# An SSD scan that keeps its outputs feature-major: decay matrix as moving side, cumulative decays spread by four products, norm by a product

## What is computed

```python
def step(h, inp):
    xc, dtc, bc, cc = inp
    cum = jnp.cumsum(dtc * a, axis=1)
    xdt = xc * dtc[..., None]
    diff = cum[:, :, None, :] - cum[:, None, :, :]
    lmat = jnp.where(tri, jnp.exp(jnp.where(tri, diff, 0.0)), 0.0)
    cb = jnp.repeat(jnp.einsum('btgn,bsgn->btsg', cc, bc), hg, axis=-1)
    y = jnp.einsum('btsh,bshp->bthp', cb * lmat, xdt) \
        + jnp.einsum('bthn,bhpn->bthp', ch, h) * jnp.exp(cum)[..., None]
    decay_out = jnp.exp(cum[:, -1:, :] - cum)
    h = h * jnp.exp(cum[:, -1])[:, :, None, None] \
        + jnp.einsum('bshn,bshp->bhpn', bh * decay_out[..., None], xdt)
    return h, y
```

## Time and profile before

| what | value |
|---|---|
| median of 3 runs | 1685.81 us (1683.71 to 1687.26) |
| the profiled execution | 1686.15 us |
| its span | 1684.3 us |
| busy in the span | PE 1557.0 (92%), DVE 771.6 (46%), ACT 629.2 (37%), POOL 421.4 (25%) |
| scan block | 836.6 to 1002.2 us of the span |
| busy in the scan block | PE 148.53, DVE 130.03, ACT 84.80, POOL 129.19 of 165.60 us |
| chunk loop | 838.0 to 966 us, then the samples |

### The profile page before, as it was taken

How to read it: one execution, slowest core, us unless ns; L and a number is a source line. 1 busy time by engine, 2 the same in 40 slices (tenths; PEclk the granted TensorE clock), 3 DMA queues, 4 the chain that set the end, 5 groups by cost and what they waited for, 6 DMA issues and landing times. The chain is left out here.

```text
span 1684.3 us, 27825 instructions
## 1 busy us (share of the span) xinstructions
PE 1557.0 (92%) x11737; PEld 1296.0 (77%) x11737; DVE 771.6 (46%) x1255; ACT 629.2 (37%) x1203; POOL 421.4 (25%) x261
## 2 busy tenths in 40 slices
PE   4899988999999899999999959998999999979897
PEld 4588766666666689999987738776999998965666
DVE  3443311465666576650098855233421422048533
ACT  4334211455555452222246543333430421226521
POOL 1142001111000022331189835121121121203422
PEclk9999998999999999999999989998999999999999
DMA  9322336412111011111110156112100135220222
...
DMA packets 125921, 129.95 MB, mean 77 GB/s; under 512 B 16824, under 2 KB 100202, under 8 KB 125670
## 3 DMA queue, kind: packets, MB, share of 16 engines
...
...
## 5 line engine op out<-in xcount | busy, mean ns | idle before, releaser
L154 PE MATMUL banks<-h_T_rest,w_ssd_high 128*128 128x352 f32 x480 | 156.0, 325 | 0.0
L154 PE MATMUL banks<-h_T_high,w_ssd_high 128*128 128x352 f32 x480 | 155.8, 325 | 0.0
L154 PE MATMUL banks<-h_T_high,w_ssd_rest 128*128 128x352 f32 x480 | 155.2, 323 | 0.0
L154 PE MATMUL banks<-out_even_w_high,mix_parts 128*128 128x512 f32 x384 | 121.9, 395 | 8.9 <-DVE out_even_w_rest L2355 8.9
L154 PE MATMUL banks<-h_T_high,w_qk_high 128*128 128x352 f32 x384 | 125.5, 327 | 0.6 <-issue 0.6
L154 PE MATMUL banks<-h_T_high,w_qk_rest 128*128 128x352 f32 x384 | 123.3, 321 | 0.0
L154 PE MATMUL banks<-h_T_rest,w_qk_high 128*128 128x352 f32 x384 | 123.2, 321 | 0.0
L1403 DVE TENSOR_REDUCE pe_T<-banks 128x1 f32<-128x512 f32 (+7 forms) x108 | 81.9, 764 | 37.4 <-PE banks L154 36.8
L1630 POOL TENSOR_TENSOR w_ssd_rest<-w_ssd,w_ssd_high 128x1024 fp32r<-128x1024 f32 x20 | 58.8, 2941 | 137.1 <-ACT w_ssd_high L1583 137.1
L154 PEld LDWEIGHTS banks<-out_even_w_high,mix_parts 128*128 128x128 f32 x384 | 73.0, 190 | 25.6 <-issue 10.4
L1320 ACT ACTIVATE p_att<-banks,pe_T 128x512 f32<-128x512 f32 (+7 forms) x128 | 86.2, 680 | 15.7 <-DVE pe_T L1403 14.8
...
## 6 DMA issues: line engine op xcount, KB each, us to landing
...
```

The source lines that it names most:

```text
L154: return nc.tensor.matmul(out, lhsT, rhs, start=start, stop=stop, skip_group_check=True)
```

## The change

Nothing else than the scan block changes, but for `S.dta`, which has a 10th column of zeros at its end.

- The decay matrix becomes the moving side of intra and x dt the stationary one, two heads of 64 features in each output tile; inter takes h as the stationary side. So y comes out feature-major, `gated_T`. exp(cum) for it is made by ScalarE from the cum banks (`from_start`, four activations of 64x512 a chunk) into `decay_from_start`, and VectorE's first product L2116 takes it as a full tile.
- The cumulative decays are spread otherwise: one product for each group of four heads makes them as rows in the cb bank; VectorE multiplies them with a pattern (`sums`, L2064) into `cum_by_head`; four products with a stationary side of ones, 32 rows each, spread them over the partitions. The mask product is gone; VectorE subtracts with a floor at zero (min with 0), in one instruction for each head, 16 of 128x128 (L2079), each with a per-partition scalar; the triangle is put into C.B by VectorE (L2066).
- z is neither turned nor copied: GpSimd gates `gated_T` with `S.zT` directly. The yT turns are gone too. x D goes into intra as eight products with diagonal matrices (made once, in front of the loop, by GpSimd).
- The norm: ScalarE squares `gated_T` (`squares`), TensorE sums it over the features with a stationary side of ones (`sum`, eight products into a 128x128 bank, which each partition then holds), VectorE scales it and takes the reciprocal, 128x128, ScalarE the root, 128x128, and `put_y` applies it in eight instructions of 128x128 (L2058) with the weight as a per-partition scalar.
- Of the weights products heads 0 to 7 stay on VectorE (L2085), heads 8 to 15 go to GpSimd (L2009).
- SyncE's loads of the samples' states wait for the gating of their chunk in place of z's turn.

```diff
-        order = [(u, 0) for u in AHEAD]
+        order = [(u, 0) for u in FIRST]
         for i in range(NTP):
-            order += [(u, i + 1) for u in AHEAD if i + 1 < NTP] if i + 1 < NTP else [("sp", 0)]
-            order += [(u, i if u != "yT" else i - 2) for u in UNITS if not (u == "yT" and i < 2)]
+            if i + 1 < NTP:
+order += [("cb", i + 1), ("xs", i + 1), ("inter", i), ("cum0", i + 1), ("cum1", i + 1)]
+            else:
+order += [("sp", 0), ("inter", i)]
+            order += [("intra", i), ("upd", i)] + ([("sum", i - 1)] if i else [])
...
+        for q in range(4):
+            mm(nc, e.ps[row(q), b, 288:288 + P], S.dta[:, i:i + 3, :].rearrange("p i h -> p (i h)")[:, 4 * q:4 * q + 32], e.F["tri"], True, True)
...
     elif u in ("cum0", "cum1"):
-        for hh in range(8):
-            hd = 8 * int(u[3]) + hh
-            mm(nc, e.ps[:, b + hh // 4, (hh % 4) * P:(hh % 4 + 1) * P], S.dta[:, i, hd:hd + 1].broadcast_to([P, P]), e.F["tri"], hh % 4 == 0, False)
-            if hh % 4 == 3:
-                last = mm(nc, e.ps[:, b + hh // 4, :].rearrange("p (h t) -> p h t", h=4), e.identb, e.B["later"][:, None, :].broadcast_to([P, 4, P]), False, True)
-    elif u == "z":
-        for j in range(8):
-            last = nc.tensor.transpose(e.ps[:, b + j // 4, (j % 4) * P:(j % 4 + 1) * P], S.zT[:, j, tok], e.ident)
+        pe.wait_ge(heads_ready, i + 1)
+        for q in (0, 1) if u == "cum0" else (2, 3):
+            last = mm(nc, e.ps[:, b + q % 2, :], ones[row(q), :], heads[row(q), :, :], True, True)
     elif u == "inter":
         pe.wait_ge(h_ready, i + 1)
-        for g in range(G):
-            last = mm(nc, e.ps[:, b + g, :], S.convT[:, 10 + g, tok], h[:, g * 512:(g + 1) * 512], True, True)
+        for j in range(8):
+            last = mm(nc, e.ps[:, b + j // 4, j % 4 * P:(j % 4 + 1) * P], h[:, j * P:(j + 1) * P], S.convT[:, 10 + j // 4, tok], True, True)
     elif u == "intra":
         pe.wait_ge(xdt_ready, i + 1)
-        for hd in range(SH):
-            if hd % 8 == 0:
-                pe.wait_ge(W_ready, 2 * i + hd // 8 + 1)
-            last = mm(nc, e.ps[:, b + hd // 8, (hd % 8) * SP_:(hd % 8 + 1) * SP_], L[:, i % 2, hd // 8, hd % 8, :],
-                      xdt[:, i % 2, hd * SP_:(hd + 1) * SP_], True, True)
+        if i == 0:
+            pe.wait_ge(d_ready, 1)
+        pe.wait_ge(W_dve, i + 1)
+        for j in range(8):
+            if j == 4:
+                pe.wait_ge(W_pool, i + 1)
+            out_j = e.ps[:, b + j // 4, j % 4 * P:(j % 4 + 1) * P]
+            mm(nc, out_j, diag_d[:, j, :], S.convT[:, j, tok], j % 4 == 0, False)
+            for x in range(2):
+                hd = 2 * j + x
+                last = mm(nc, out_j[x * SP_:(x + 1) * SP_, :], xdt[:, i % 2, hd * SP_:(hd + 1) * SP_], L[:, i % 2, hd // 8, hd % 8, :], False, j % 4 == 3)
...
-    elif u == "yT":
-        pe.wait_ge(yn_ready, i + 1)
+    elif u == "sum":
+        pe.wait_ge(y_squared, i + 1)
         for j in range(8):
-            last = nc.tensor.transpose(e.ps[:, b + j // 4, (j % 4) * P:(j % 4 + 1) * P], y[:, i % 3, j * P:(j + 1) * P], e.ident)
...
+    nc.scalar.activation(sm[:, i % 2, 1:3, :], sm[:, i % 2, 1:3, :], ACT.Exp).then_inc(decays, 1)
+def from_start(i):
+    if i >= 2:
+        act.wait_ge(taken["inter", "dve"], i - 1)
+    for c in range(2):
+        act.wait_ge(done[f"cum{c}"], i + 1)
+        src = both(f"cum{c}", i).rearrange("p b (j x t) -> p (b j) x t", x=2, t=P)
+        for x in range(2):
+            half = slice(x * SP_, (x + 1) * SP_)
+            last = nc.scalar.activation(E[half, i % 2, c * 512:(c + 1) * 512].rearrange("p (j t) -> p j t", j=4), src[half, :, x, :], ACT.Exp)
+        last.then_inc(taken[f"cum{c}", "act"], 1)
...
-def gate_rows(i):
-    act.wait_ge(done["z"], i + 1)
-    nc.scalar.copy(zs[:, i % 2, :].rearrange("p (b n) -> p b n", b=2), both("z", i)).then_inc(taken["z", "act"], 1)
-def norm(i):
+def squares(i):
     act.wait_ge(y_gated, i + 1)
-    nc.scalar.activation(zs[:, i % 2, :], y[:, i % 3, :], ACT.Square, accum_out=ss[:, i % 2, :]).then_inc(y_squared, 1)
+    if i:
+        act.wait_ge(done["sum"], i)
+    nc.scalar.activation(sq, y[:, i % 3, :, :], ACT.Square).then_inc(y_squared, 1)
+def root(i):
     act.wait_ge(var_ready, i + 1)
     nc.scalar.activation(ss[:, i % 2, :], ss[:, i % 2, :], ACT.Sqrt).then_inc(std_ready, 1)
-    act.wait_ge(std_ready, i + 1)
-    nc.scalar.activation(y[:, i % 3, :], y[:, i % 3, :], ACT.Copy, scale=ss[:, i % 2, :]).then_inc(yn_ready, 1)
...
 copies(0)
+from_start(0)
+decay(0)
 for i in range(NTP):
     if i + 1 < NTP:
         copies(i + 1)
     else:
         sample_copies()
-    gate_rows(i)
     if i:
-        norm(i - 1)
+        squares(i - 1)
+    if i + 1 < NTP:
+        from_start(i + 1)
+        decay(i + 1)
+    if i >= 2:
+        root(i - 2)
 act.wait_ge(done["out"], 1)
-act.wait_ge(y_gated, NTP - 1)
-nc.scalar.copy(zs[:, 0, :].rearrange("p (b n) -> p b n", b=2), both("out", 0)).then_inc(taken["out", "act"], 1)
+nc.scalar.copy(E[:, 0, :].rearrange("p (b n) -> p b n", b=2), both("out", 0)).then_inc(taken["out", "act"], 1)
+squares(NTP - 1)
...
+def weights(i):
+    k = i % 2
+    pool.wait_ge(L_ready, 2 * i + 2)
+    nc.gpsimd.tensor_tensor(L[:, k, 1, :, :], L[:, k, 1, :, :], cc[:, k, P:2 * P][:, None, :].broadcast_to([P, 8, P]), ALU.mult).then_inc(W_pool, 1)
...
-    yi = y[:, i % 3, :]
+    yi = y[:, i % 3, :, :]
     pool.wait_ge(taken["intra", "dve"], i + 1)
-    link(nc.gpsimd.tensor_tensor(yi, yi, xsb[:, i % 3, :], ALU.add))
-    pool.wait_ge(taken["z", "act"], i + 1)
-    nc.gpsimd.tensor_tensor(yi, yi, zs[:, i % 2, :], ALU.mult).then_inc(y_gated, 1)
+    nc.gpsimd.tensor_tensor(yi, yi, S.zT[:, :, i * P:(i + 1) * P], ALU.mult).then_inc(y_gated, 1)
...
-def put_yT(i):
-    dve.wait_ge(done["yT"], i + 1)
-    s = VEC["ssd_norm"][0]
-    nc.vector.tensor_tensor(S.convT[:, 0:8, i * P:(i + 1) * P], both("yT", i).rearrange("p b (j t) -> p (b j) t", j=4),
-                            e.vec[:, s:s + 8][:, :, None].broadcast_to([P, 8, P]), ALU.mult).then_inc(taken["yT", "dve"], 1)
 def variance(i):
-    dve.wait_ge(y_squared, i + 1)
-    link(nc.vector.tensor_scalar(ss[:, i % 2, :], ss[:, i % 2, :], 1.0 / SI, EPS, ALU.mult, ALU.add))
+    dve.wait_ge(done["sum"], i + 1)
+    nc.vector.tensor_scalar(ss[:, i % 2, :], e.ps[:, pair[("sum", i)], 0:P], 1.0 / SI, EPS, ALU.mult, ALU.add).then_inc(taken["sum", "dve"], 1)
+    dve.wait_ge(taken["sum", "dve"], i + 1)
     nc.vector.reciprocal(ss[:, i % 2, :], ss[:, i % 2, :]).then_inc(var_ready, 1)
+def put_y(i):
+    dve.wait_ge(std_ready, i + 1)
+    for j in range(8):
+        nc.vector.scalar_tensor_tensor(S.convT[:, j, i * P:(i + 1) * P], y[:, i % 3, j, :], e.vec[:, norm_w + j:norm_w + j + 1], ss[:, i % 2, :], ALU.mult, ALU.mult)
+def sums(i):
+    k = i % 2
+    dve.wait_ge(done["cb"], i + 1)
+    b = pair[("cb", i)]
+    nc.vector.tensor_tensor(heads[:, :, :], e.ps[:, b, 288:288 + P][:, None, :].broadcast_to([P, 4, P]), e.F["fold"][:, 0:4][:, :, None].broadcast_to([P, 4, P]), ALU.mult).then_inc(heads_ready, 1)
+    nc.vector.tensor_copy(cc[:, k, 256:288], e.ps[:, b, 256:288])
+    nc.vector.tensor_tensor(cc[:, k, 0:256].rearrange("p (g t) -> p g t", g=G), e.ps[:, b, 0:256].rearrange("p (g t) -> p g t", g=G),
+                            e.F["tri"][:, None, :].broadcast_to([P, G, P]), ALU.mult).then_inc(taken["cb", "dve"], 1)
+    dve.wait_ge(taken["cb", "dve"], i + 1)
+    nc.vector.tensor_copy(sm[:, k, 2, :], cc[:, k, 272:288])
+    nc.vector.tensor_tensor(sm[:, k, 1, :], cc[:, k, 272:288], cc[:, k, 256:272], ALU.subtract).then_inc(small, 1)
 def differences(i):
     k = i % 2
-    dve.wait_ge(done["cb"], i + 1)
-    nc.vector.tensor_copy(cc[:, k, :], e.ps[:, pair[("cb", i)], 0:288]).then_inc(taken["cb", "dve"], 1)
-    dve.wait_ge(taken["cb", "dve"], i + 1)
-    nc.vector.tensor_copy(sm[:, k, 0, :], cc[:, k, 256:272])
-    nc.vector.tensor_copy(sm[:, k, 2, :], cc[:, k, 272:288])
-    nc.vector.tensor_tensor(sm[:, k, 1, :], cc[:, k, 272:288], cc[:, k, 256:272], ALU.subtract).then_inc(small, 1)
     for c in range(2):
         dve.wait_ge(done[f"cum{c}"], i + 1)
-        nc.vector.tensor_tensor(L[:, k, c, :, :], both(f"cum{c}", i).rearrange("p b (h t) -> p (b h) t", h=4),
-                                cc[:, k, 256 + 8 * c:264 + 8 * c][:, :, None].broadcast_to([P, 8, P]), ALU.subtract).then_inc(taken[f"cum{c}", "dve"], 1)
-def weights(i, c):
+        dve.wait_ge(taken[f"cum{c}", "act"], i + 1)
+        src = both(f"cum{c}", i).rearrange("p b (h t) -> p (b h) t", h=4)
+        for x in range(8):
+            last = nc.vector.tensor_scalar(L[:, k, c, x, :], src[:, x, :], cc[:, k, 256 + 8 * c + x:257 + 8 * c + x], 0.0, ALU.subtract, ALU.min)
+        last.then_inc(taken[f"cum{c}", "dve"], 1)
...
+def weights(i):
     k = i % 2
-    dve.wait_ge(L_ready, 2 * i + c + 1)
```

(52 more changed lines are left out.)

52 lines of the change are left out of this document (28 added, 24 removed).

## The result

The changed kernel takes 1737.2 us (median of 4 runs, 1735.39 to 1741.67) against 1686.11 us: 1.031 times, 95% interval 1.029 to 1.033. Forecast were 1715 us and a range up to 1726: the direction holds, the size is 51 us where 29 were forecast.

The account below looks back on a forecast made before the run. TensorE, VectorE and GpSimd were close together before; VectorE's longer chain would set the pace after. Five intervals +28.2, first two +3, head -3.5 and tail +1 gave +28.7 on 1686.15: 1715 us, range 1692 to 1726.

Parts of the forecast that it names:

- What bounds the kernel before: Old chunk loop: TensorE busy 15.39 of 16.03 us, VectorE and GpSimd close behind; VectorE loses 3.1 us to GpSimd.
- VectorE's chain: One steady chunk, from one inter product to the next: VectorE's instructions and waits together 20.95 us.
- the clock term: Steady chunk: inter and cum products run partly at TensorE's lower clock after it idles, 0.9 us, making 21.85.
- put_y with its three waits: Steady chunk: eight products, 2.2 us, with three GpSimd products slipping in between, waits of 1.8 + 2.3 + 1.8.
- Rivals 1 and 2: put_y: only the first product waits, 1694.5 us, chance 0.15; or three-input form doesn't wait at all, 1685.5 us, chance 0.05.
- rival 3: Loop: VectorE and GpSimd seldom meet and the clock stays, period 14.1 us, total 1672.5 us, chance 0.10.
- I put its work at 12.7 us a chunk against 15.: TensorE in a chunk: work falls to 12.7 us, so it stops being the bound unless its clock falls.
- I charge 0.9 us a chunk.: Steady chunk: inter and cum products at the lower TensorE clock for about half their time on VectorE's path.
- The last interval: End of the loop: no weights, no sums, one GpSimd product less, but the samples' differences; 18.5 us.
- Rival 4: Loop: TensorE stays at 1.2 GHz and bounds it with 23 to 25 us a chunk; 1733 us, chance 0.05.
- Head, first two, tail: Around the steady part: one weights product less, -3.5; two intervals without put_y, +3; put_y three times at the end, +1.
- The cold pass: Loop: a skill's rule that waits put TensorE's clock down every pass, so each starts cold; used to support 0.9 us.

Follow-up runs that it names:

- run 1: The changed kernel with six extra 512-column TensorE products, results overwritten, in the gap ahead of cum0 of chunks 4 to 7: 1713.9 us.
- run 4: The changed kernel with intra's eight diagonal products placed first, then the sixteen products of the heads, in place of alternating: 1705.8 us.

## Why the prediction was wrong, step by step

- *What bounds the kernel before, and VectorE's chain.* Right. Without the clock term the sum was 20.95 us; the chunk with TensorE kept warm (run 1) has 21.15. That it is so close is in part luck: it has waits for TensorE of 0.83 and 0.68 us that the sum lacks, and lacks the wait of 0.95 for GpSimd's product of weights. Differences, pitch, reciprocal and put_y with its three waits (8.1 forecast, 7.57 measured) came out within 7%. Rivals 1 and 2 fall by put_y's 7.57, rival 3 by the period.
- *"I put its work at 12.7 us a chunk against 15."* The first step that failed. It is 15.4 us: intra was priced at some 3.5 us (eight D products at 1.75, the pairs of heads side by side at about as much) and took 6.3, since full-width and half-width products alternate. Grouped they need 4.0 at full clock.
- *"I charge 0.9 us a chunk."* The term that was mis-sized: 6.3 us. The gap, its cause and the fall of the clock were as told (a gap of 5.7 us, not over 8), but I let only cum and inter run slowly. Cum's part measured 0.95 us and inter runs at full clock; intra and upd, which I put at nothing, run slowly too and cost 4.5 and 0.8. At 10.8 us no cover is left for intra (VectorE's differences take 4.2). Run 1 shows the term, run 4 that it hangs on intra: with 3.5 us doubled to 7 intra would have ended some 1.4 us behind the differences in place of 5.4 (an estimate from the rows of the steady chunk), so the first step made most of the second. Of the 26 us missing in the five intervals, 0.3 fall on the first, 16.8 on the three that follow, 8.9 on the last; the head and the first two take 4 back, which leaves the 22 by which 51 exceeds 29.
- *The last interval*, 18.5 forecast, 27.4 measured. Some 2.1 us of this is a misreading of the program: weights(7) stands in it. The rest is mostly the clock: kept warm, this interval takes 20.1.
- *Rival 4*, given 0.05 at 1733 us, had the total but not the picture. TensorE doesn't bound the loop, it idles 5.7 us in it; the clock comes back in each chunk, too late.
- *Head, first two, tail*: -5.8, +1.4 and +1.4 against -3.5, +3 and +1. The head lies outside its bounds of -1 and -4, and the first two depend on the clock: run 1 has 5.5 us more there.
- *The cold pass.* The Trainium skill's rule of a loop that starts each pass cold ("TensorE: Matmul & The Clock Gate", section "HAM oscillation — how this bites in real kernels") is what these rows show: after 5.72 us of idling the cum products take 2.19 us where run 1 has 1.24, in every steady chunk. I quoted it and then priced it by the shortest products.
